# A causal depthwise convolution on TensorE: four taps per product in 32-column tiles instead of two in 64-column tiles

## What is computed

```python
def conformer_conv(x, w_in, b_in, conv_w, conv_b, ln_g, ln_b, w_out, b_out):
    a, g = jnp.split(x @ w_in + b_in, 2, axis=-1)
    h = a * jax.nn.sigmoid(g)
    h = lax.conv_general_dilated(
        h, conv_w[:, None, :].astype(h.dtype), window_strides=(1,),
        padding=[(CONV_KERNEL - 1, 0)],
        dimension_numbers=("NWC", "WIO", "NWC"),
        feature_group_count=D_MODEL) + conv_b
    h = jax.nn.silu(layer_norm(h, ln_g, ln_b))
    return h @ w_out + b_out
```

## Time and profile before

| | |
|---|---|
| runs | 1450.88 us median of 3 (1450.86, 1450.88, 1453.41) |
| profiled execution | span 1449.6 us, from the first instruction to the last |
| instructions | 19954 |
| busy in the span | TensorE 99%, VectorE 64%, ScalarE 44%, GpSimd 14% |
| convolution stage | about 933 to 1045 us of the span |
| granted TensorE clock | full in every slice |

### The profile page before, as it was taken

One profiled execution on the slowest core, in us unless ns is written; L12 is line 12 of the kernel. 1 busy time (PEld: TensorE's weight loads), 2 busy tenths in 40 slices (PEclk: granted clock), 3 DMA queues, 4 the chain that ended last, 5 costly groups with the idle time before them and its releaser, 6 DMA issues.

```text
span 1449.6 us, 19954 instructions
## 1 busy us (share of the span) xinstructions
PE 1438.0 (99%) x6828; PEld 1172.4 (81%) x6828; DVE 920.6 (64%) x1339; ACT 636.6 (44%) x994; POOL 204.9 (14%) x162
## 2 busy tenths in 40 slices
PE   9999999999999999999999999999999999999999
PEld 8788888888877898888888888766588888888887
DVE  7877773573645667776754755899988653544532
ACT  7444442342536675444432434798754322222210
POOL 4100000000302232000000003599611000000000
PEclk9999999999999999999999999999999999999999
DMA  5223233233322012333232232387613332232321
GB/s 191 88 93 110 87 102 116 73 102 90 121 87 73 30 60 73 101 102 102 87 118 86 87 102 87 102 178 186 160 45 102 114 102 88 98 104 89 102 94 51
DMA packets 44414, 144.34 MB, mean 100 GB/s; under 512 B 5185, under 2 KB 6209, under 8 KB 44353
## 3 DMA queue, kind: packets, MB, share of 16 engines
q1 hardware_dynamic: 41200, 133.79, 28.4%
q0 software_dynamic: 2016, 7.34, 2.8%
q10 hardware_dynamic: 1136, 2.42, 0.4%
HBM read 137.19 MB, written 2.10 MB: 96 GB/s over the span
## 4 chain that ended last, share of the span: by engine, by line
PE 93%; DVE 3%; ACT 1%; DMA 1%; issue 1%; POOL 1%; SPq 0%; ACTq 0%; DVEq 0%; POOLq 0%
PE bank L586 29%; PE bank L588 28%; PE bank L587 28%; PE bank L860 2%; PE bank L734 1%; PE bank L762 1%; PE bank L747 1%; DVE bank L1682 1%; DMA cst<-cst_in 1%; PE bank L870 0%; DMA shifted<-hc 0%; DVE wlo L1333 0%; PE bank L915 0%; PE bank L916 0%; PE bank L627 0%
## 5 line engine op out<-in xcount | busy, mean ns | idle before, releaser
L586 PE MATMUL bank<-xh,whi 128*128 128x512 f32 x1184 | 464.9, 393 | 1.6 <-DVE res L1621 0.7
L588 PE MATMUL bank<-xh,wlo 128*128 128x512 f32 x1184 | 460.9, 389 | 0.0
L587 PE MATMUL bank<-xl,whi 128*128 128x512 f32 x1184 | 460.8, 389 | 0.0
L938 ACT ACTIVATE whi<-raw 128x1024 fp32r<-128x1024 f32 x244 | 255.8, 1050 | 237.4 <-PE bank L588 234.7
L1333 DVE TENSOR_TENSOR wlo<-raw,whi 128x1024 fp32r<-128x1024 f32 x230 | 287.9, 1252 | 43.9 <-ACT whi L938 35.9
L586 PEld LDWEIGHTS bank<-xh,whi 128*128 128x128 f32 x1184 | 222.2, 188 | 56.0 <-issue 7.1
L587 PEld LDWEIGHTS bank<-xl,whi 128*128 128x128 f32 x1184 | 222.3, 188 | 46.7 <-issue 1.2
L588 PEld LDWEIGHTS bank<-xh,wlo 128*128 128x128 f32 x1184 | 222.2, 188 | 46.5
L586 PE MATMUL bank<-ahi,whi 128*128 128x512 f32 x608 | 236.5, 389 | 0.0
L587 PE MATMUL bank<-alo,whi 128*128 128x512 f32 x608 | 236.5, 389 | 0.0
L588 PE MATMUL bank<-ahi,wlo 128*128 128x512 f32 x608 | 236.5, 389 | 0.0
(11 more groups left out here) (191 smaller groups left out, 1343.3 us busy)
## 6 DMA issues: line engine op xcount, KB each, us to landing
raw<-w_ffn_up SPq DMA_DIRECT2D x88, 512.0 KB, 3.3
raw<-w_ffn_down SPq DMA_DIRECT2D x32, 512.0 KB, 3.3
raw<-w_mlp_up SPq DMA_DIRECT2D x32, 512.0 KB, 3.3
raw<-w_mlp_down SPq DMA_DIRECT2D x32, 512.0 KB, 3.3
raw<-w_ain SPq DMA_DIRECT2D x16, 512.0 KB, 3.5
raw<-w_ffn_down SPq DMA_DIRECT2D x16, 384.0 KB, 3.0
raw<-w_qkv SPq DMA_DIRECT2D x12, 512.0 KB, 3.3
wlo<-w_ain POOLq DMA_DIRECT2D x10, 512.0 KB, 7.4
```

Source lines behind the costliest of these rows:

```text
L586: nc.tensor.matmul(out_, hi, mh, start=first, stop=False)
L587: nc.tensor.matmul(out_, hi, ml, start=False, stop=False)
L588: return nc.tensor.matmul(out_, lo, mh, start=False, stop=last)
L938: nc.scalar.activation(whi[:, s, 0:tiles * P], raw[:, s, 0:tiles * P], ACT.Copy)\
```

## The change

One convolution product now handles four taps of 32 features for chunks 0 to 6: four copies of 32 rows stacked to 128 contracted rows, four tiles of 32 columns for the 128 outputs; a chunk needs 16 DMAs for its copies. Chunk 7 keeps two taps and 64 columns, with four DMAs. The diagonals are made on VectorE, one multiplication of broadcast views for a chunk, and there are two buffers of them instead of three. The norm sums are made in four tiles of 32 columns by 256 tokens. Taps move between the engines: 86 instead of 68 on TensorE, 65 instead of 72 on ScalarE and GpSimd, 97 instead of 108 on VectorE. The tap weights come in 26 small DMAs instead of 6. The table of the accumulating loads (`LOW_AT`) and the places of a few splits on ScalarE move by a step.

```diff
-PE_TAPS = (8, 6, 6, 4, 6, 6, 14, 18)
-SHIFTS = 2
-GROUP = P // SHIFTS
+PE_TAPS = (8, 8, 8, 8, 8, 12, 20, 14)
+SHIFTS = (4, 4, 4, 4, 4, 4, 4, 2)
+GROUP = tuple(P // s for s in SHIFTS)
+ROUNDS = tuple(n // s for n, s in zip(PE_TAPS, SHIFTS))
...
-DIAGS = 3
-POOL_TAPS = (11, 10, 9, 9, 9, 9, 8, 7)
-LATE_TAPS = (0, 6, 8, 11, 11, 12, 4, 0)
-LATE_START = (2, 2, 2, 0, 0, 0, 0, 4)
+DIAGS = 2
+POOL_TAPS = (10, 9, 9, 8, 8, 8, 7, 6)
+LATE_TAPS = (2, 4, 6, 9, 12, 9, 0, 0)
+LATE_START = (2, 2, 2, 0, 0, 0, 0, 0)
...
             def load_pairs():
...
+                for shifts, (lo, hi) in SPREAD.items():
+                    group = P // shifts
+                    for s in range(shifts):
+                        rows = slice(s * group, (s + 1) * group)
+                        sp.dma_start(pair_id[shifts][rows, :], cst_in[0:group, i:i + group]).then_inc(pairs_loaded, 16)
+                        for g in range(shifts):
+                            src = vec_in[g * group:(g + 1) * group, w:w + C * TAPS].rearrange("p (c k) -> p c k", c=C)
+                            sp.dma_start(pair_w[shifts][rows, g], src[:, lo:hi, s:s + PAIR_TAPS[shifts]])\
+                                .then_inc(pairs_loaded, 16)
...
             def shift_hc(c):
...
-                for g in range(SHIFTS):
-                    for s in range(SHIFTS):
-                        sp.dma_start(shifted[s * GROUP:(s + 1) * GROUP, c % 2, g, 0:n],
-                                     hc[g * GROUP:(g + 1) * GROUP, c % HC, s:s + n]).then_inc(hc_shifted[c % 2], 16)
+                for g in range(SHIFTS[c]):
+                    for s in range(SHIFTS[c]):
+                        sp.dma_start(shifted[s * group:(s + 1) * group, c % 2, g, 0:n],
+                                     hc[g * group:(g + 1) * group, c % HC, s:s + n]).then_inc(hc_shifted[c % 2], 16)
...
             def convolve(c):
...
-                pairs = PE_TAPS[c] // SHIFTS
-                for q in range(pairs):
-                    for g in range(SHIFTS):
-                        mm = nc.tensor.matmul(bank[6 + b][g * GROUP:(g + 1) * GROUP, :], dg[:, c % DIAGS, q, g, :],
-                                              shifted[:, b, g, SHIFTS * q:SHIFTS * q + T],
-                                              start=(q == 0), stop=(q == pairs - 1))
+                for q in range(ROUNDS[c]):
+                    for g in range(SHIFTS[c]):
+                        rows, at = slice(g * group, (g + 1) * group), SHIFTS[c] * q
+                        mm = nc.tensor.matmul(bank[6 + b][rows, :], dg[:, c % DIAGS, q, rows],
+                                              shifted[:, b, g, at:at + T],
+                                              start=(q == 0), stop=(q == ROUNDS[c] - 1))
...
             def statistics(c):
...
+                for j, x in enumerate((hv[:, c, :], sq[:, c % 2, :])):
+                    for h in range(2):
+                        rows, at = slice((2 * j + h) * QUADRANT, (2 * j + h + 1) * QUADRANT), slice(h * T // 2, (h + 1) * T // 2)
+                        mm = nc.tensor.matmul(norm[0][rows, at], ones[:, 0:QUADRANT], x[:, at],
+                                              start=(c == 0), stop=(c == C - 1))
...
+            def diagonals(c):
+
+                if c >= DIAGS:
+                    dve.wait_ge(conv_done, c - DIAGS + 1)
...
+                V.tensor_tensor(dg[:, c % DIAGS, 0:rounds].rearrange("p q (g n) -> p q g n", g=shifts),
+                                pair_id[shifts][:].rearrange("p (q g n) -> p q g n", q=1, g=1).broadcast_to(shape),
+                                w.rearrange("p g (q n) -> p q g n", n=1).broadcast_to(shape), ALU.mult)\
+                    .then_inc(diag_ready, 1)
...
                 if c < C - 1:
                     gated(c)
+                diagonals(c)
```

More of the change, by code:

```diff
@@ L204, in build @@
             stat = sb("stat", [P, 6, NBLK * KV, REP], F32, own)
-            pair_w = sb("pair_w", [P, SHIFTS, C * TAPS], F32, own)
-            pair_id = sb("pair_id", [P, GROUP], F32, own)
+            pair_w = {s: sb(f"pair_w{s}", [P, s, b - a, PAIR_TAPS[s]], F32, own) for s, (a, b) in SPREAD.items()}
+            pair_id = {s: sb(f"pair_id{s}", [P, P // s], F32, own) for s in SPREAD}
         with ExitStack() as own:
@@ L212, in build @@
             hc = sb("hc", [P, HC, TAPS - 1 + T], F32, own)
-            dg = sb("dg", [P, DIAGS, max(PE_TAPS) // SHIFTS, SHIFTS, GROUP], F32, own)
+            dg = sb("dg", [P, DIAGS, max(ROUNDS), P], F32, own)
             tapped = sb("tapped", [P, PARTS, T], F32, own)
-            shifted = sb("shifted", [P, 2, SHIFTS, max(PE_TAPS) - SHIFTS + T], F32, own)
+            shifted = sb("shifted", [P, 2, max(SHIFTS), max(PE_TAPS) - min(SHIFTS) + T], F32, own)
         sb("overlay", [P, OVERLAY])
@@ L851, in convolve @@
             def convolve(c):
-                b = c % 2
-                pe.wait_ge(hc_shifted[b], 16 * SHIFTS * SHIFTS * (c // 2 + 1))
+                b, group = c % 2, GROUP[c]
+                pe.wait_ge(hc_shifted[b], 16 * sum(SHIFTS[e] ** 2 for e in range(b, c + 1, 2)))
                 pe.wait_ge(diag_ready, c + 1)
@@ L869, in statistics @@
                 pe.wait_ge(hv_squared, c + 1)
-                nc.tensor.matmul(norm[0][0:GROUP, :], ones[:, 0:GROUP], hv[:, c, :],
-                                 start=(c == 0), stop=(c == C - 1))
-                nc.tensor.matmul(norm[0][GROUP:P, :], ones[:, 0:GROUP], sq[:, c % 2, :],
-                                 start=(c == 0), stop=(c == C - 1)).then_inc(stats_done, 1)
+                for j, x in enumerate((hv[:, c, :], sq[:, c % 2, :])):
[3 more added lines that the diff above has]
+                                              start=(c == 0), stop=(c == C - 1))
+                mm.then_inc(stats_done, 1)
             for c in range(C):
@@ L897, in _ @@
             for b in range(NBLK):
+                i = CST_ID + QUADRANT * (b // 2)
                 mm = nc.tensor.matmul(norm[1][:, 2 * b:2 * b + 2], token_sums_of[:, b * P:(b + 1) * P],
-                                      cst[:, CST_ID:CST_ID + P:GROUP], start=True, stop=True)
+                                      cst[:, i:CST_ID + P:2 * QUADRANT], start=True, stop=True)
             mm.then_inc(sqsum_done, 1)
@@ L1211, in _ @@
             p = ph["ain"]
-            def diagonals(c, part=0, parts=1):
-                if c >= DIAGS and part == 0:
-                    act.wait_ge(conv_done, c - DIAGS + 1)
-                if c == 0:
-                    act.wait_ge(pairs_loaded, 16 * SHIFTS * (SHIFTS + 1))
-                pairs = PE_TAPS[c] // SHIFTS
-                for q in range(part * pairs // parts, (part + 1) * pairs // parts):
-                    e = c * TAPS + SHIFTS * q
-                    for g in range(SHIFTS):
-                        last = nc.scalar.activation(dg[:, c % DIAGS, q, g, :], pair_id[:], ACT.Copy,
-                                                    scale=pair_w[:, g, e:e + 1])
-                if part == parts - 1:
-                    last.then_inc(diag_ready, 1)
             def products(c, ks):
@@ L1749, in _ @@
                 gate_at = next((n for n in range(rounds) if issued[n] >= GATE_AT), rounds - 1)
-                gated_at = next((n for n in range(rounds) if issued[n] >= LAST_GATED), rounds - 1)
                 for n in range(rounds):
@@ L1756, in _ @@
                         evict(c + 1, 0)
-                    if n == gated_at and c == C - 2:
-                        gated(C - 1)
                     if n < len(own):
@@ L1764, in _ @@
                     collect(c - 1)
+                if c == C - 2:
+                    gated(C - 1)
             collect(C - 1)
```

63 lines of the change are left out of this document (27 added, 36 removed).

## The result

The changed kernel takes **1460.98 us** (median of 4 runs, 1460.54 to 1463.18), the kernel before 1451.20 beside it (4 runs, 1450.86 to 1453.41): a ratio of 1.0069 (95% interval 1.0057 to 1.0081), 10 us slower. The forecast was 1454.8. The sign was right, the size was not. The profiled execution has a span of 1459.0 us, 9.4 more than the one of before.

The account below looks back on a forecast made before the run. TensorE, busy 99% of the span, was taken to bound the kernel, VectorE and DMA close behind; waits for copies use up its saving. Span 1449.6 + 3.9 (later stage end) + 1.3 (median offset) = 1454.8 us; range 1446.0 to 1461.0.

Parts of the forecast that it names:

- TensorE's work: Second block's convolution: rounds of four tiles take 0.86 us, sums 0.43; TensorE's path to the last convolution 9.8 us shorter.
- rival of separate tiles: Convolution rounds: four tiles do not overlap, 15 us more on TensorE less hidden waits, about 1464 us; chance 0.04.
- Issues: SyncE's queue: each copy DMA takes 0.64 us from start to start, for 32 rows as well.
- The rival with 0.24 of the chance: SyncE's copies: issue cost falls with the rows, 0.32 us a DMA, giving 1447.2 us; chance 0.24.
- Landing, 11.9 and 13.6 us: From gated chunk to 16 copies landed: 11.9 us for chunk 0, 13.6 for later chunks beside accumulating loads.
- The recurrence: Convolution stage, chunk by chunk: gating, copies, convolution and chains advance 14.3 us a chunk; stage ends about 3.9 us later.
- 7: gated 1034.4, four copies, down 1038.6: Chunk 7: copies land 4.2 us after gating, its convolution starts at 1038.8 and ends at 1044.9.
- The clock, 2.5 us: First convolution: after standing idle 6.4 us TensorE returns at its lower clock, losing 2.5 us.
- the clock holds: First convolution: TensorE keeps its clock through the 6.4 us wait, 2.5 us less, about 1452.7 us; chance 0.14.
- 0.43 us for most chunks: VectorE's new broadcast multiplication: 0.43 us for most chunks, 4.6 in all; with fewer taps VectorE gains 3 to 4 us.
- ScalarE and the tap tables: Removed scalings, 17.1 us, worth nothing; 26 small loads delay the first weight load's landing to 387.6, cost 0.
- The DMA engines fill up: Copies: doubled bytes make landing 15.3 us, every second chunk waits 1.7 us more, 1458.8 us; chance 0.20.

Follow-up runs that it names:

- experiment 1: The kernel before, with each chunk's four copies (chunks 0 to 6) cut into 16 DMAs of 16 rows, same bytes: 1461.7 us, ratio 1.0076.
- experiments 8 and 9: Changed kernel, GpSimd's accumulating loads cut to 8 KB: the first with 4 copies of 128 rows a chunk, 1450.0 us; the second with 16 copies, 1453.1 us.
- experiment 2: The changed kernel with chunk 7's four copies issued ahead of the two weight loads: 1459.9 us, ratio 1.0073.
- experiment 3: The changed kernel with 26 unused products filling TensorE's wait for chunk 0's copies: 1464.5 us, ratio 1.0102.
- Experiment 12: The kernel before with ScalarE's 68 scalings replaced by one broadcast multiplication a chunk on VectorE: 1461.5 us, ratio 1.0074.
- Experiment 11: The changed kernel with 4 copies of 128 rows a chunk, but chunks 0 and 1 in two 64-column tiles with 2 copies each: 1455.3 us, ratio 1.0029.

## Why the prediction was right and wrong

**TensorE's work: right.** A round of four tiles takes 0.87 us against the 0.86 taken, the sums 0.43. The bound of 1.71 and the rival of separate tiles fall. The ratio of 2.38 for three column tiles, weighed there from the Trainium skill, "TensorE: Matmul & The Clock Gate", Part 3, does not show for these four fp32 tiles of 32 columns: by the estimate made from it there, a round would have taken 1.08 us.

**Issues: right.** 0.63 us from start to start for 32 rows and for 16. The rival with 0.24 of the chance is refuted. The rule weighed there, in the Trainium skill, "DMA: Bandwidth & Descriptors", Rules for kernel authors, is that transfers under 64 KB are mostly overhead. The copies here have 64.5 KB, just over it, and those of experiment 1 have 32 KB, at the same spacing: that agrees.

**Landing, 11.9 and 13.6 us: right.** Chunk 0 measured 11.6, chunks 1 to 6 14.4, 13.4, 14.8, 13.8, 13.9 and 12.7, mean 13.8. The prediction had both parts in it, 11.9 us by the count and the rest by the loads; experiments 8 and 9 show them one by one.

**The recurrence held up to chunk 6.** Convolution starts, forecast against measured: 945.0 and 944.2, 960.4 and 959.4, 975.5 and 974.5, 989.0 and 989.1, 1004.1 and 1003.5, 1017.5 and 1018.2, 1033.9 and 1033.1.

**The step that failed is its last line,** "7: gated 1034.4, four copies, down 1038.6". The gating came at 1034.5, as forecast. But 4.2 us to landing was the time of four copies with nothing ahead of them. It measured 9.0 us. Two statements of the prediction stand behind the 4.2, each priced at nothing. The one on the copies had seen that two weight loads stand behind 16 copies and start later, and gave "Cost 0" because ScalarE could wait; it did not ask who stands behind the loads, which is chunk 7. Before, chunk 7's copies were issued from 1028.43, some 8 us after the two loads ahead of them; now two loads of 512 KB went out 2.9 and 2.3 us ahead. The other said that GpSimd's accumulating loads come one step earlier, "which changes nothing that TensorE waits for". `LOW_AT` moved one of them from chunk 7's additions to chunk 6's, from behind chunk 7's copies to 2.9 us ahead of them.

The traces show that it takes both:

| ahead of chunk 7's four copies | L, us |
|---|---|
| nothing for 8 us (before) | 4.2 |
| two weight loads, 2.7 and 3.6 us (experiments 1 and 9) | 4.6, 4.6 |
| GpSimd's load, 2.9 us (experiment 2) | 5.2 |
| both, 2.9 us (changed kernel; experiment 3) | 9.0, 7.5 |

Each row is one or two executions, of kernels that differ otherwise too. That GpSimd's load alone, put back to its old place, would have saved the changed kernel from this wait is likely from the second row; no run tried it.

The convolution started 4.7 us later than forecast, and the idle time brought a second fall of the clock, which the sum didn't have: 8.3 us instead of 6.1. Together the reciprocal started at 1052.6 and not at 1046.9, 5.7 us, nearly all of the 6.2 us between forecast and measurement.

**The clock, 2.5 us: right in size, wrong in place.** The first convolution took 1.7 us more and the chains behind it ran 0.5 us over, but experiment 3's trace shows that this was hidden by chunk 1's copies. The rival "the clock holds" came out 2.1 us lower for it (1452.7); in that trace it is worth 0.3 us at most. The fall that counts is the one at the end, behind which nothing waits for copies.

**VectorE: right at the end, wrong as to its margin.** Without the wait for chunk 7, VectorE would have ended at 1046.8 (1046.1 and a collection of 0.7), against 1046.9 forecast. But "0.43 us for most chunks" holds only while GpSimd is not adding, and the prediction priced the multiplication by its length alone. Experiment 12 shows its price by position: ahead of TensorE's next low parts it costs 5 us. In the changed kernel the same order stands, and the split ran 2.34 us instead of 1.22, to 948.1. It went unseen because TensorE, whose convolution had waited for its copies until 944.2 and ended at 947.8, asked for it only then. Experiment 11 took the copies' wait away and met it.

**ScalarE and the tap tables: right.** ScalarE's splits waited 23.3 us for weights, and no gating was late by it. The first attention weights were split at 384.97 instead of 383.73, under cover. The forecast was 387.6: the 26 small issues stood 0.53 us apart in the mean and not 0.64.

**"The DMA engines fill up": half right.** Its 1458.8 us is nearest to the measurement, but by another way. It had every second chunk wait 1.7 us more; the chunks came on the forecast's times. What is true of it is the table of experiments 8 and 9: GpSimd's loads are worth as much as the issues. The doubled bytes of the copies, which it had in mind, are worth less: 0.1 us of L for chunk 0 and some 1.5 us for the others (experiment 1 against the changed kernel).

## What to carry to other kernels

When a change lengthens a burst in an in-order queue, follow the queue one item further than the burst: what was moved behind it now stands ahead of the next urgent transfer. Look at the other queues at the same moment, too: here two plain loads ahead cost 0.4 us, another queue's load 1.0, and both together 4.8. Cutting a copy into more pieces costs its count times the issue time, and whether that is hidden depends on the other traffic; price the two together, since either alone may cost little. And removing work from the leading engine is worth at most the distance to the next one: here 9.8 us of products were worth 1.7 us, even with few copies and small loads.

## What the runs showed of the hardware

- In the changed kernel, a VectorE operation with both inputs in SBUF that met a running addition of GpSimd was held until that addition ended. The split at 945.75 met one with 1.25 us left and took 2.34 us instead of 1.22. Sums of 512 elements (0.69 us alone) met ones with 0.53, 0.76 and 0.82 us left and took 1.08, 1.31 and 1.37. The extra time is each time what was left, less 0.12 to 0.14 us. A multiplication of 384 elements took 0.56 us alone (experiment 11), and 1.19 (changed kernel) and 1.99 (experiment 12) beside additions. The Trainium skill, "SBUF — State Buffer", Who interferes with whom, says that a VectorE instruction with two SBUF inputs contends with a GpSimd instruction that reads SBUF. These traces agree, and scalar_tensor_tensor taps, with one input in PSUM, stayed at 0.73 to 0.76 us.
- SyncE's issue of a copy takes 0.59 us in a row of them, for 16, 32, 64 or 128 rows; four copies of 264 KB in a row took 0.6 us first and up to 1.7 and 2.7 us later. It is no constant: a weight load issued by itself took 0.33 us, and the tap tables' later issues 0.44. What sets it was not looked into.
- 512 KB loads that accumulate, in flight beside the copies, raised the median landing from 2.0 to 3.8 us and single issues from 0.59 to 1.9 us (chunks 0 and 1 of the changed kernel). With these loads cut to 8 KB no issue of chunk 1 took over 0.59 us.
- Of 20 stops of TensorE of 2.3 to 6.1 us in this stage, in all profiled executions together, 18 had the clock fall to 1.2 GHz, inside the stop or right behind it: 9 for 6.8 us (stops of 3.2 to 6.1 us) and 9 for 3.4 us (2.3 to 5.9 us); behind two (2.8 and 3.4 us) it held. So a stop of given length has no fixed price; at half the clock, 6.8 us cost at most 3.4 us of TensorE's work.
- Where waits for copies decide, runs of one kernel spread: 1456.1 to 1469.2 (experiment 2) and 1459.6 to 1471.0 (experiment 3), against 1450.7 to 1453.4 of the kernel before; the changed kernel itself had 1460.5 to 1463.2. Medians of four or five such runs don't tell 3 us apart.
